# Completing the chunk inverse of a gated delta rule on 64x64 blocks, two tiles per visit, and moving those visits

## The reference

```python
a_mat = jnp.where(strict, beta[..., :, None] * kk * decay, 0.0) + jnp.eye(CHUNK)   # 64 x 64, unit lower triangular
rhs = jnp.concatenate([v * beta[..., None], k * (beta * jnp.exp(G))[..., None]], axis=-1)
sol = lax.linalg.triangular_solve(a_mat, rhs, left_side=True, lower=True, unit_diagonal=True)
...
def step(state, inp):
    v_new = u_c - w_c @ state
    o_c = qd_c @ state + qk_c @ v_new
    state = state * cd_c + kd_c^T @ v_new
```

## Time and profile before

| | us |
|---|---|
| median of 3 executions | 668.57 |
| profiled execution | 667.52 |
| its span, first to last instruction | 665.8 |
| TensorE busy in the span | 635.4 |
| VectorE busy | 477.3 |
| ScalarE busy | 393.6 |

### The profile page before, as it was taken

How to read it: one execution, slowest core, us unless ns; L and a number is a source line. 1 busy time by engine, 2 the same in 40 slices (tenths; PEclk the granted TensorE clock), 3 DMA queues, 4 the chain that set the end, 5 groups by cost and what they waited for, 6 DMA issues and landing times.

```text
span 665.8 us, 9330 instructions
## 1 busy us (share of the span) xinstructions
PE 635.4 (95%) x3396; PEld 525.9 (79%) x3397; DVE 477.3 (72%) x808; ACT 393.6 (59%) x670; POOL 171.3 (26%) x216
## 2 busy tenths in 40 slices
PE   7999999968899999999999998999999999999985
PEld 6788878756688898888888886788888888888863
DVE  5778995367622534425664658899999999999877
ACT  7448584246635142244342463388899888998753
POOL 7000007995000000000000000234747546556100
PEclk9999999998999999999999999799999999999998
DMA  9556535203422222222325954268687876985673
GB/s 279 189 168 191 128 80 156 66 6 79 128 64 64 64 63 64 64 64 74 116 67 202 388 195 159 56 199 276 207 284 242 277 278 219 295 260 174 234 272 127
DMA packets 76960, 108.51 MB, mean 163 GB/s; under 512 B 31863, under 2 KB 54464, under 8 KB 76786
## 3 DMA queue, kind: packets, MB, share of 16 engines
q1 hardware_dynamic: 64320, 99.76, 46.4%
q0 software_dynamic: 12480, 8.11, 4.1%
q10 hardware_dynamic: 114, 0.04, 0.0%
HBM read 123.90 MB, written 20.98 MB: 218 GB/s over the span
## 4 chain that ended last, share of the span: by engine, by line
PE 85%; DVE 8%; DMA 2%; ACT 2%; issue 1%; SPq 0%; POOLq 0%; DVEq 0%; ACTq 0%
PE bank L1748 22%; PE bank L1750 22%; PE bank L1749 22%; PE bank L2201 3%; DMA expert_rows<-expert_rows_hbm 1%; PE bank L1816 1%; PE bank L1998 1%; PE bank L1988 1%; DVE rank_onehot L1586 1%; ACT w_hi L810 1%; DVE probs L1319 1%; DVE y_T L1718 1%; PE bank L2119 1%; DMA x_T<-in_x 1%; PE bank L2217 1%
## 5 line engine op out<-in xcount | busy, mean ns | idle before, releaser
L1748 PE MATMUL bank<-h_hi,w_hi 128*128 128x512 f32 x288 | 117.7, 409 | 0.0
L1750 PE MATMUL bank<-h_hi,w_lo 128*128 128x512 f32 x288 | 113.0, 392 | 0.0
L1749 PE MATMUL bank<-h_lo,w_hi 128*128 128x512 f32 x288 | 112.7, 391 | 0.0
L1466 DVE TENSOR_TENSOR gate_up_lo<-ew_raw,gate_up_hi 128x1024 fp32r<-128x1024 f32 x92 | 108.4, 1218 | 1.8 <-ACT gate_up_hi L1018 1.8
L1135 DVE TENSOR_TENSOR w_lo<-w_raw,w_hi 128x2048 fp32r<-128x2048 f32 x26 | 59.8, 2300 | 52.1 <-ACT w_hi L810 52.1
L742 POOL DMA_INDIRECT unit_tokens<-ffn_rows,row_index x23 | 27.8, 1207 | 266.1 <-DVE row_index L1594 255.1
L1018 ACT ACTIVATE gate_up_hi<-ew_raw 128x1024 fp32r<-128x1024 f32 x92 | 92.1, 1051 | 0.9 <-DMA ew_raw<-in_w_up,extra_weight_rows 0.9
L1748 PE MATMUL bank<-gate_up_hi,unit_in_hi 128*128 128x512 f32 x184 | 75.9, 413 | 0.2 <-DVE unit_in_lo L1620 0.2
L1750 PE MATMUL bank<-gate_up_hi,unit_in_lo 128*128 128x512 f32 x184 | 72.1, 392 | 0.0
L1749 PE MATMUL bank<-gate_up_lo,unit_in_hi 128*128 128x512 f32 x184 | 71.9, 391 | 0.0
L1748 PEld LDWEIGHTS bank<-h_hi,w_hi 128*128 128x128 f32 x288 | 54.5, 189 | 12.0 <-issue 2.2
(11 more groups left out here) (396 smaller groups left out, 1300.3 us busy)
## 6 DMA issues: line engine op xcount, KB each, us to landing
w_raw<-in_w_in SPq DMA_DIRECT2D x16, 1024.0 KB, 5.2
ew_raw<-in_w_gate SPq DMA_DIRECT2D x32, 512.0 KB, 6.1
ew_raw<-in_w_up SPq DMA_DIRECT2D x32, 512.0 KB, 6.3
ew_raw<-in_w_down SPq DMA_DIRECT2D x32, 512.0 KB, 5.3
expert_rows_hbm<-sub_product SPq DMA_DIRECT2D x16, 256.0 KB
w_raw<-in_w_out SPq DMA_DIRECT2D x4, 1024.0 KB, 5.1
expert_rows<-expert_rows_hbm SPq DMA_DIRECT2D x8, 512.0 KB, 7.2
x_T<-in_x SPq DMA_DIRECT2D x4, 512.0 KB, 5.0
```

What stands on the lines that cost most here:

```text
L1466: dve.tensor_tensor(dst, eraw[slot][:, :], hi.bitcast(F32), ALU.subtract).then_inc(elo_done, 1)
L1748: pe.matmul(out_ap, lhs_hi, rhs_hi, start=first, stop=False)
L1749: pe.matmul(out_ap, lhs_hi, rhs_lo, start=False, stop=False)
L1750: return pe.matmul(out_ap, lhs_lo, rhs_hi, start=False, stop=last)
```

## The change

`low_inverse`, `inv_add`, `low_inv` and `level` no longer take one tile but two (tiles 0 and 1, or 2 and 3), and the matmuls work on 64x64 blocks. A block that lies in partitions 0 to 63 or 64 to 127 uses only that half of the array's rows, and a result that goes to PSUM partitions 0 to 63 or 64 to 127 only that half of its columns. The first level multiplies the two diagonal blocks of each tile and head; its second product needs only 32 of its columns. The wide level multiplies one block of each tile and head. `low_inv_T` has a new layout (two tiles, 4 heads, 64 columns).

The visits stand in other places. Both tiles 0 and 1 are inverted ahead of the recurrence, with the same table of side steps. Tiles 2 and 3 are turned in steps 0 and 1; their levels run in step 1 and at the head of step 2. VectorE's first level for them stands behind the normalisation in step 1, and its wide level behind `v_less_state` in step 2. The tables `PRE_STEPS` and `STEPS` are as before.

```diff
-            def level(n_, wide):
-                dve.wait_ge(turned, n_ + 1)
-                dve.wait_ge(e_ps, 2 * n_ + wide + 1)
...
+            def level(two, wide):
+                dve.wait_ge(turned, 2 * two + 2)
+                dve.wait_ge(e_ps, 2 * two + wide + 1)
+                if wide:
+                    for i in range(2):
+                        ins = dve.tensor_scalar(invT[i][half_tile(0), :, P // 2:], bank_of_pair(3)[half_tile(0), i, :, :], -1.0, None, ALU.mult)
+                else:
+                    for q in range(0, P, 2 * BLOCK):
+                        lo_, up = slice(q, q + BLOCK), slice(q + BLOCK, q + 2 * BLOCK)
+                        dve.tensor_scalar(inv[up, 2 * two:2 * two + 2, :, lo_], bank_of_pair(4)[up, :, :, 0:BLOCK], -1.0, None, ALU.mult)
+                        for i in range(2):
+                            ins = dve.tensor_scalar(invT[i][lo_, :, up], bank_of_pair(3)[lo_, i, :, 0:BLOCK], -1.0, None, ALU.mult)
...
@@ VectorE, step m
+                if m == 2:
+                    level(1, 1)
...
-                    level(n_, 0)
                 side_splits(steps_at(m, 4))
...
                 dve.tensor_tensor(d_on[:, :, :], bank4(7), bc_last(ors[:, :], P), ALU.mult).then_inc(on_done, 1)
+                if m == 1:
+                    level(1, 0)
                 if n_ < TT:
-                    level(n_, 1)
@@ TensorE
+            def low_inverse(two, wide):
+                for i in range(2):
+                    for h in range(HA):
+                        for q in range(1 if wide else 2):
+                            rows_ = half_tile(1 if wide else q)
+                            ins = pe.matmul(bank_of_pair(2)[half_tile(q), i, h, :], low[rows_, 2 * two + i, h, half_tile(q)],
+                                            invT[i][rows_, h, rows_], start=True, stop=True)
...
+            def inv_add(two, wide):
...
+                        if wide:
+                            d = half_tile(0)
+                            ins = pe.matmul(bank_of_pair(3)[d, i, h, :], inv[d, n_, h, d], d_x[d, i, h, :], start=True, stop=True)
+                        else:
+                            for q in range(2):
+                                d = half_tile(q)
+                                pe.matmul(bank_of_pair(4)[d, i, h, 0:BLOCK], d_x[d, i, h, :],
+                                          inv[d, n_, h, 2 * BLOCK * q:2 * BLOCK * q + BLOCK], start=True, stop=True)
+                            for q in range(2):
+                                d = half_tile(q)
+                                ins = pe.matmul(bank_of_pair(3)[d, i, h, 0:BLOCK], inv[d, n_, h, d], d_x[d, i, h, BLOCK:],
+                                                start=True, stop=True)
...
             inv_turn(0)
             side(PRE_STEPS[0] // 2)
+            pe.wait_ge(turned, 1)
+            inv_turn(1)
...
@@ TensorE, step m
+                if m == 2:
+                    inv_add(1, 1)
                 side(STEPS[m][0])
...
-                if more:
-                    pe.wait_ge(turned, n_ + 1)
-                    low_inverse(n_)
+                if m < 2:
+                    if m:
+                        pe.wait_ge(turned, 3)
+                    inv_turn(m + 2)
...
-                if more:
-                    if m:
-                        pe.wait_ge(oaf_done, m)
-                    inv_add(n_, 0)
+                if m == 1:
+                    pe.wait_ge(turned, 4)
+                    low_inverse(1, 0)
                 side(STEPS[m][3])
-                if more:
-                    pe.wait_ge(level_done, 2 * n_ + 1)
-                    low_inverse(n_)
+                if m == 1:
+                    pe.wait_ge(oaf_done, m)
+                    inv_add(1, 0)
                 side(STEPS[m][4])
-                if more:
-                    inv_add(n_, 1)
+                if m == 1:
+                    pe.wait_ge(level_done, 3)
+                    low_inverse(1, 1)
                 side(STEPS[m][5])
```

More of the change, by code:

```diff
@@ L165, in build @@
         inv = at("inv", [P, TT, HA, P], F32, r_g + 16384)
-        d_s, d_x, d_r, d_vn = (at(n_, [P, HA, P], F32, r_b + o) for n_, o in
-                               (("state", 0), ("low_inv_T", 2048), ("v_less_state", 8192), ("v_new_T", 10240)))
+        d_s, d_r, d_vn = (at(n_, [P, HA, P], F32, r_b + o) for n_, o in
+                          (("state", 0), ("v_less_state", 8192), ("v_new_T", 10240)))
+        d_x = at("low_inv_T", [P, 2, HA, P // 2], F32, r_b + 2048)
         d_v = [at(f"v_beta_T{i}", [P, HA, P], F32, r_b + 4096 + 2048 * i) for i in range(2)]
@@ L555, in steps_at, with bank_of_pair, half_tile @@
             return sum(PRE_STEPS) + sum(sum(v) for v in STEPS[:m]) + sum(STEPS[m][:n_])
+        def bank_of_pair(b):
+            return ps[b][:, :].rearrange("p (i h c) -> p i h c", i=2, h=HA)
+        def half_tile(q):
+            return slice(P // 2 * q, P // 2 * (q + 1))
         def turn_back_bank(m):
@@ L960, in _ @@
             inv_turned(0)
+            inv_turned(1)
             low_inv(0)
@@ L971, in _ @@
                 act.activation(d_vn[:, :, :], bank4(6), ACT.Copy).then_inc(vn_done, 1)
-                if n_ < TT:
-                    low_inv(2 * n_)
+                if m < 2:
+                    inv_turned(m + 2)
                 if m:
@@ L1367, in v_beta @@
                 dve.tensor_tensor(d_v[n_ % 2][:, :, :], bank4(5), bc_last(bv[:, n_, :], P), ALU.mult).then_inc(v_done, 1)
-            def level(n_, wide):
-                dve.wait_ge(turned, n_ + 1)
-                dve.wait_ge(e_ps, 2 * n_ + wide + 1)
-                b = 64 if wide else BLOCK
-                for q in range(0, P, 2 * b):
-                    lo_, up = slice(q, q + b), slice(q + b, q + 2 * b)
-                    if not wide:
-                        dve.tensor_scalar(inv[up, n_, :, lo_], bank4(4)[up, :, lo_], -1.0, None, ALU.mult)
-                    ins = dve.tensor_scalar(invT[n_ % 2][lo_, :, up], bank4(3)[lo_, :, up], -1.0, None, ALU.mult)
+            def level(two, wide):
[3 more added lines that the diff above has]
+                    for i in range(2):
+                        ins = dve.tensor_scalar(invT[i][half_tile(0), :, P // 2:], bank_of_pair(3)[half_tile(0), i, :, :], -1.0, None,
+                                                ALU.mult)
+                else:
[4 more added lines that the diff above has]
+                            ins = dve.tensor_scalar(invT[i][lo_, :, up], bank_of_pair(3)[lo_, i, :, 0:BLOCK], -1.0, None, ALU.mult)
                 ins.then_inc(level_done, 1)
@@ L1983, in v_turn @@
                 ins.then_inc(v_ps, 1)
-            def low_inverse(n_):
-                for h in range(HA):
-                    ins = pe.matmul(bank4(2)[:, h, :], low[:, n_, h, :], invT[n_ % 2][:, h, :], start=True, stop=True)
+            def low_inverse(two, wide):
[5 more added lines that the diff above has]
+                                            invT[i][rows_, h, rows_], start=True, stop=True)
                 ins.then_inc(lx_ps, 1)
-            def inv_add(n_, wide):
-                pe.wait_ge(lx_done, 2 * n_ + wide + 1)
-                if not wide:
+            def inv_add(two, wide):
+                pe.wait_ge(lx_done, 2 * two + wide + 1)
+                for i in range(2):
+                    n_ = 2 * two + i
                     for h in range(HA):
-                        pe.matmul(bank4(4)[:, h, :], d_x[:, h, :], inv[:, n_, h, :], start=True, stop=True)
-                for h in range(HA):
-                    ins = pe.matmul(bank4(3)[:, h, :], inv[:, n_, h, :], d_x[:, h, :], start=True, stop=True)
+                        if wide:
[10 more added lines that the diff above has]
+                                                start=True, stop=True)
                 ins.then_inc(e_ps, 1)
@@ L2007, in _ @@
             side(PRE_STEPS[0] - PRE_STEPS[0] // 2)
-            pe.wait_ge(turned, 1)
-            low_inverse(0)
+            pe.wait_ge(turned, 2)
+            low_inverse(0, 0)
             side(PRE_STEPS[1])
@@ L2013, in _ @@
             pe.wait_ge(level_done, 1)
-            low_inverse(0)
+            low_inverse(0, 1)
             side(PRE_STEPS[3])
@@ L2033, in _ @@
                 side(STEPS[m][1])
-                pe.wait_ge(level_done, 2 * m + 2)
+                pe.wait_ge(level_done, 2 * (m // 2) + 2)
                 if m:
```

13 lines of the change are left out of this document (7 added, 6 removed).

## The result

The change makes the kernel slower by 0.6%: 673.36 us (671.8 to 675.76, 10 runs) against 669.3 us (668.09 to 671.41, 10 runs) for the kernel before, timed beside it. The ratio is 1.006, with a 95% interval of 1.0045 to 1.0076, so about 4.1 us. The prediction had the sign and 1.4 us of it; the time lies above its range of 666.6 to 673.0.

What follows compares the result with a forecast made beforehand. TensorE was taken to bound the kernel (85% of the chain of waits). Its path went from 18.5 to 18.2 us (-0.3); with 1.7 for the clock's fall, +1.4 on 668.57 gave 670.0 us, range 666.6 to 673.0.

Steps and rivals of the forecast that it cites:

- the sign: Whole kernel: slower by 1.4 us with the clock's fall; without that fall, 0.3 us faster.
- visit with 16 records in a position: TensorE, both `low_inverse` and the wide `inv_add`: 16 x 0.056 + 0.36 = 1.26 us each, six of them.
- first `inv_add`: TensorE, first level of each pair of tiles: 32 x 0.056 + 0.36 = 2.15 us each, two of them.
- first wait: Ahead of tile 1's transposes, about 183.6 us: TensorE waits 1.3 us for ScalarE's copy of tile 0.
- second wait: Step 1, ahead of `low_inverse(1, 1)`: TensorE waits 5.0 us for VectorE's first level, now behind the normalisation.
- sum against before, no clock: TensorE's path: 18.2 us where 18.5 stood before, 0.3 us less, with both waits counted.
- saving if TensorE never waited: TensorE's visits for the inverse: 11.9 us together instead of 17.8, 5.9 us saved.
- the load of weights sets the pace: TensorE's small records: load, not streaming, sets the time; 0.056 us per record of 64 weight columns in its position.
- Positions that take turns: First-level visits: two positions writing to one PSUM bank alternate; +3.3 us, 671.9 us; chance 0.13.
- Cheaper records at 0.027: 64x64 visits: records of one position overlap at 0.027 us; -3.1 us, 665.5, or 667.2 with the clock's fall; chance 0.12.
- The clock that holds through the wait: Long wait in step 1: same waits, no clock loss; -0.3 us, 668.3 us; chance 0.20.
- the clock's price: Behind the long wait in step 1: clock falls to half speed, 1.7 us lost, between nothing and 3.4.

Runs made afterwards that it cites:

- e4: Changed kernel with 20 matmuls that nobody reads filling TensorE's long wait in step 1; 670.15 us, ratio 0.9994 to the kernel before.
- e3: Changed kernel with VectorE's first level of tiles 2 and 3 ahead of the split and tile 1's transposes in their own PSUM bank; 664.07 us, ratio 0.9917.
- e1: Changed kernel with VectorE's first level of tiles 2 and 3 moved ahead of the split and normalisation in step 1; 666.81 us, ratio 0.9948.
- e0: The changed kernel again, with no edit; 675.32 us, ratio 1.0076 to the kernel before.
- e2: Changed kernel with tile 1's transposes in PSUM bank 3 instead of 2, without TensorE's wait for tile 0's copy; 670.36 us, ratio 1.0002.
- e6: Changed kernel with tile 1's transposes in their own bank and 6 unread matmuls where the first wait was; 673.25 us, ratio 1.0045.
- e9: Changed kernel with 6 instead of 12 unread matmuls in the router; 673.7 us, ratio 1.0058 to the kernel before.
- e5: Kernel before, its order and one tile per visit kept, with only the 64x64 blocks of the change; 667.92 us, ratio 0.996.
- e7: Changed kernel with tile 1's transposes in their own bank and 11 unread matmuls where the first wait was; 673.77 us, ratio 1.005.
- e8: The kernel before again, with no edit; 670.66 us, ratio 1.001.

## Why the prediction was right in its sign and short in its size

**TensorE's list: right.** The sum held term by term.

| term | predicted | measured |
|---|---|---|
| visit with 16 records in a position | 1.26 | 1.26 to 1.27 |
| first `inv_add` | 2.15 | 2.18 |
| first wait | 1.3 | 1.31 |
| second wait | 5.0 | 4.9 |
| sum against before, no clock | -0.3 | -0.3 (e4: 125.94 against 126.25) |
| saving if TensorE never waited | 5.9 | 5.75 (e3: 5.95, less 0.2 of the shorter wait) |

The step that the load of weights sets the pace, from the router's rows and the shorter load of 64 columns, gave the right price; the visits with 32 and with 64 streamed columns show that the streaming does not set it. The second wait came out of a chain on ScalarE and VectorE read from the trace of before, and of instructions counted in the new order; that it would be later than anything TensorE has left was the step that used up the saving. e1 shows it from the other side: with the level ahead of the split the wait is gone. The sign itself came from the clock: without its fall the sum is -0.3, and e4's recurrence is that case. The prediction gave the fall a chance of one half, so part of the right sign is luck.

**The rivals.** Positions that take turns: refuted, 32 records in two positions last as long as 16 in one. The rule named with it ("TensorEngine Tiling (Array Packing)" in the Trainium skill, Restrictions and Gotchas) cost nothing here for two diagonal positions that write to different partitions of one bank: 1.27 us for both against 1.26 for one. Whether the two write at the same moment, or take turns in time that the weight loads leave, no run shows. Cheaper records at 0.027: refuted, 0.057. The clock that holds through the wait: literally true in the first profile, and of no use, since it fell in the moment that the wait ended (in e0 0.35 us, in e2 2.3 us ahead of it). What I had not split there is "holds through the wait" and "holds behind it".

**The failed step: the clock's price.** I took 1.7 us, between nothing and 3.4, reasoning from the earlier trace rows that a shorter wait leaves a shorter low stretch behind it. Measured are 3.1 us (e4). The low stretch did not shrink with the wait, it was 6.8 us long again; what changed was how much of it fell into the wait. In the earlier trace rows 2.6 us of it did and 2.1 us were lost; in e2 2.3 us did; in the changed kernel, e0 and e6 0.4 us or less did, and almost the whole upper bound was paid. A shorter wait leaves more of the stretch outside, so the argument pointed the wrong way. This is 1.4 us of the miss.

**The step that was missing: the router.** I wrote that a microsecond more or less between 181 and 308 us should arrive whole at the end. I put the code behind 308 us at nothing and did not ask what else a later program meets: TensorE's list was 3.1 us late at that mark, and the end was 4.2 us late in the spans. The second low stretch ahead of the experts cost 1.15 us. It is there in the profiles of the changed kernel, e0, e4, e6 and e9, and not in those of before, e2, e3, e5, e7 and e8; e1 has one half as long, and the one behind it 3.4 us longer, together worth 0.34. With 1.4 + 3.1 - 1.7 = 2.8 for the recurrence and 1.15 for the router the change comes to 3.95 us, against 4.1 measured. The rest of the distance to the predicted 670.0 is the level of the comparison, in which the kernel before ran at 669.3 instead of 668.57.

**What stays open.** Why the clock falls in the router in some kernels and not in others is not settled. The fall in the recurrence is neither needed for it nor enough (e4's profile has the one without the other, those of e2 and e7 the other without the one), nor is lateness as such (e7's profile reaches the router later than e6's and is spared). It is no fixed property of a kernel either: the mean clocks say that the changed kernel, e0, e6 and e9 had it in nearly every run, e4 in some, and five of e7's ten runs had a mean clock low enough for it. So it seems to hang on how an execution lies against the clock's own changes; that is argued, not shown. A profile is one execution, and of each experiment there is one; e0, e1, e2 and e4 also have a low stretch of 3.4 us at 42 to 47 us, long ahead of the changed code, that the other profiles lack.

## What to carry to other kernels

When a change pairs or delays work, list for each wait of the busiest engine what stands ahead of the releaser on the releaser's own engine: here six short VectorE operations (2 us) behind a split and a normalisation (5.3 us) turned a saving of 5.9 us into none, and putting them first, with a bank of its own for a second transpose, gave it all back. Price an idle stretch of about 5 us on TensorE at the whole low stretch that the trace shows elsewhere, not at the part that happened to be paid there, and look in the clock row for new dips far from the change. Where a wait can't be removed, unread matmuls in it kept the clock up here (e4), worth 3.1 us; with the same trick in the router, begun when the clock was already low, they delayed what they were to help.

## What the runs showed of the hardware that I had not expected

- The same wait, 4.9 us long, cost 3.1 us of clock where the fall met its end (255.11 against 255.18) and about 2.1 where the fall came 2.3 us earlier (e2). A shift by 1.4 us of busy work moved it from the one to the other (e6).
- Two 64x64 positions on the diagonal that write to one PSUM bank lost no time to each other: 32 records in a visit of 1.27 us, 16 in one of 1.26.
- With 64 weight columns of f32 a record takes 0.057 us in its position, at 32 streamed columns as at 64.
- In the router 12 bf16 matmuls of 512 columns took 4.56 us, the clock low for the first 3.6 of them, and 2.54 at the full clock (11 of the 12 are in that trace); a stretch meant to hold the clock up became the thing that was waited for.
- Mean granted clocks of single runs tell how often a low stretch comes: 0.973 to 0.976 in all ten runs of the changed kernel, 0.978 to 0.986 in e4's twelve, whose profile is the 0.978.
